# V stationary and two heads on column halves, with the probabilities normalised by GpSimd before they are turned

## The reference

```python
# first block
h = rms_norm(x); qa, ka, va, qb, kb, vb, ga, gb, mg = split(h @ w_in)
ya = banded_attention(qa, ka, va, 128, 1, bias_a, sink) * silu(ga)    # 8 heads, 2 of k and v
yb = sum(alpha[g] * dilated_group(qb[g], kb[g], vb[g]) for g in 3) * silu(gb)   # 8 heads, 3 groups
x = x + (gates[0] * (ya @ w_branch_a) + gates[1] * (yb @ w_branch_b)) @ w_out
# each of two layers
o_nsa  = gs[0] * o_compressed + gs[1] * o_selected + gs[2] * o_window  # 8 heads of 64
o_ret  = silu(g_r) * layernorm(retention(q_r, k_r, v_r)) * gn
o_conv = silu(layernorm(conv31(c_a * sigmoid(c_b))))
x = x + sum(sigmoid(m_g[i]) * (o[i] @ w_branch[i]) for i in 3) @ w_out
x = x + relu(rms_norm(x) @ w_ff1)**2 @ w_ff2
```

## Time and profile before

| | us |
|---|---|
| median of 3 runs (lowest, highest) | 1196.53 (1196.03, 1196.99) |
| the profiled execution | 1196.16 |
| its span, first to last instruction | 1194.4 |
| TensorE busy in it | 1165.7 (98%) |
| VectorE busy | 826.1 (69%) |
| ScalarE busy | 571.1 (48%) |
| GpSimd busy | 46.1 (4%) |

### The profile page before, as it was taken

One profiled execution on the slowest core, in us unless ns is written; L12 is line 12 of the kernel. 1 busy time (PEld: TensorE's weight loads), 2 busy tenths in 40 slices (PEclk: granted clock), 3 DMA queues, 4 the chain that ended last, 5 costly groups with the idle time before them and its releaser, 6 DMA issues.

```text
span 1194.4 us, 17220 instructions
## 1 busy us (share of the span) xinstructions
PE 1165.7 (98%) x6879; PEld 1008.8 (84%) x6879; DVE 826.1 (69%) x1317; ACT 571.1 (48%) x701; POOL 46.1 (4%) x56
## 2 busy tenths in 40 slices
PE   7999999999999999999999999999999999999996
PEld 5888788887898787888999888998778878999885
DVE  4666466557679888787767554699889686777442
ACT  5655565443435666543534433525756534434331
POOL 0232000000000001000000000000000000000000
PEclk9999999999999999999999999999999999999999
DMA  9557555347546666754555565546667654555640
GB/s 310 209 175 247 212 150 177 94 141 264 177 145 211 207 157 191 215 184 161 179 189 178 202 209 178 176 153 214 180 175 214 199 176 147 207 180 188 214 141 36
DMA packets 41344, 219.73 MB, mean 184 GB/s; under 512 B 4311, under 2 KB 14039, under 8 KB 16615
## 3 DMA queue, kind: packets, MB, share of 16 engines
q1 hardware_dynamic: 39104, 204.62, 49.2%
q0 software_dynamic: 1824, 13.78, 6.2%
q10 hardware_dynamic: 336, 0.22, 0.1%
HBM read 217.41 MB, written 1.20 MB: 183 GB/s over the span
## 4 chain that ended last, share of the span: by engine, by line
PE 88%; DVE 4%; ACT 2%; DMA 2%; issue 2%; DVEq 1%; POOLq 0%; POOL 0%; ACTq 0%
PE panel L923 19%; PE panel L925 18%; PE panel L924 18%; PE panel L946 7%; PE panel L945 7%; PE panel L944 7%; PE tile L973 4%; DMA ring_parts<-in_w_layers_dram 2%; DVE ring_parts L613 1%; PE heads_out L1134 1%; ACT ring_parts L571 1%; PE panel L963 1%; PE panel L962 1%; PE panel L961 1%; ACT ring_parts L573 0%
## 5 line engine op out<-in xcount | busy, mean ns | idle before, releaser
L613 DVE TENSOR_TENSOR ring_parts<-ring,ring_parts 128x2048 fp32r<-128x2048 f32 (+1 forms) x173 | 388.1, 2255 | 155.9 <-ACT ring_parts L571 144.6
L571 ACT ACTIVATE ring_parts<-ring 128x2048 fp32r<-128x2048 f32 (+1 forms) x185 | 348.4, 1889 | 260.6 <-PE panel L925 202.3
L923 PE MATMUL panel<-ring_parts,hT_high 128*128 128x512 f32 (+2 forms) x688 | 280.1, 407 | 5.5 <-DMA ring_parts<-in_w_layers_dram 2.4
L925 PE MATMUL panel<-ring_parts,hT_low 128*128 128x512 f32 (+2 forms) x688 | 265.6, 386 | 0.0
L924 PE MATMUL panel<-ring_parts,hT_high 128*128 128x512 f32 (+2 forms) x688 | 264.9, 385 | 0.0
L944 PE MATMUL panel<-hT_high,ring_parts 128*128 128x256 f32 x704 | 199.4, 283 | 0.0
L946 PE MATMUL panel<-hT_high,ring_parts 128*128 128x256 f32 x704 | 199.2, 283 | 0.0
L945 PE MATMUL panel<-hT_low,ring_parts 128*128 128x256 f32 x704 | 199.2, 283 | 0.0
L923 PEld LDWEIGHTS panel<-ring_parts,hT_high 128*128 128x128 f32 x688 | 130.1, 189 | 37.9 <-issue 11.5
L925 PEld LDWEIGHTS panel<-ring_parts,hT_low 128*128 128x128 f32 x688 | 129.9, 189 | 26.9
L923 PE MATMUL panel<-ring_parts,area_parts 128*128 128x512 f32 x384 | 150.6, 392 | 0.0
(11 more groups left out here) (235 smaller groups left out, 1113.9 us busy)
## 6 DMA issues: line engine op xcount, KB each, us to landing
ring<-in_w_layers_dram SPq DMA_DIRECT2D x140, 1024.0 KB, 4.9
ring<-in_w_first_dram SPq DMA_DIRECT2D x40, 1024.0 KB, 5.0
ring_parts<-in_w_layers_dram POOLq DMA_DIRECT2D x12, 1024.0 KB, 8.9
area<-bias_rows SPq DMA_DIRECT2D x16, 160.0 KB, 3.1
ring<-in_w_layers_dram SPq DMA_DIRECT2D x4, 560.0 KB, 3.8
area<-bias_rows SPq DMA_DIRECT2D x16, 96.0 KB, 3.0
area<-bias_rows SPq DMA_DIRECT2D x1, 1536.0 KB, 8.7
area<-in_gains_dram SPq DMA_DIRECT2D x3, 512.0 KB, 5.7
```

Source lines behind the costliest of these rows:

```text
L571: act.activation(ring_lo[:, SLOTS + hi, 0:w], ring[:, slot, 0:w], ACT.Copy).then_inc(high_ready, 1)
L613: g.tensor_tensor(ring_lo[:, slot, 0:w], ring[:, slot, 0:w], ring_lo[:, SLOTS + hi, 0:w], ALU.subtract).then_inc(low_ready, 1)
L923: pe.matmul(ps[:, b, 0:width], high, hi[:, k, :], start=first, stop=False)
L925: mm = pe.matmul(ps[:, b, 0:width], low, hi[:, k, :], start=False, stop=last)
```

## The change

It moves the attention of both kinds to another form, and rewrites both plans.

- *Products.* `outputs_first` and `outputs_layer` do one pair at a time. V is stationary (64 columns), the turned probabilities of up to 256 tokens move, and head i of the pair writes the 64 partitions from 64 i of `heads_out`, now 2 x 256 columns: the output is already turned. `open_group` opens each group with a matmul of zeros over all 512 columns; every product adds to it. A group is 2 pairs in the first block and 4 pairs in a layer, where the selected and window heads of the same four heads and the compressed outputs (`compressed_out(i)`, step O) add to one sum.
- *Normalisation.* GpSimd computes 1/sum by a power, multiplies by the gate (layer) or the row's scale (first block) and scales the probabilities in place, before they are turned. In the first block VectorE scales every second B head (`scale_odd`). TensorE's T waits for `scaled` or `scaled_by_v`. `L` has four slots.
- *Gates and outputs.* In the first block the gates of ga and gb are turned instead of the outputs (step g), kept in x, and multiplied in (`gated_outputs`); x is loaded again later. In a layer step h makes the high and low parts straight from `heads_out`; step y is gone, `sum_out` and `normed_out` too. The compressed probabilities are scaled by VectorE before they are turned (step cmpN).
- *Retention.* Its outputs go to two tiles (Or0, Or1), ScalarE keeps them in SBUF, and VectorE normalises from there. Panels Oc and Or are gone.
- *Order.* In the first block the panel ga moves ahead of vb1, and the wide stage is vb1, vb2, gb, mg0 to mg3: 56 chunks. All chunks of all steps are written out in tables. GpSimd's queue holds scalings and `add_low` in turns (`LOW_ADDED_AT`). The eviction of a wide panel in the first block is done behind chunk 1 of the next.

The diff, cut to its core:

```diff
+FIRST_S = ((0,), (3,), (8,), (12,), (16, 17), (23, 25), (30, 32), (37, 39))
+FIRST_E = (3, 7, 10, 13, 20, 27, 32, 41)
+FIRST_T = ((5, 5), (10, 10), (14, 15), (20, 20), (26, 26), (31, 33), (39, 39), (46, 47))
+FIRST_V = (7, 14, 16, 21, 27, 39, 41, 48)
+FIRST_GATES, FIRST_HIGH = (7, 14, 35, 37), (22, 23, 43, 51)
+LAYER_S = (0, 4, 11, 18, 25, 28, 37, 44)
+LAYER_E = (2, 5, 15, 22, 29, 33, 43, 49)
+LAYER_T = (6, 14, 19, 27, 33, 41, 47, 54)
+LAYER_V = (8, 15, 22, 30, 37, 44, 49, 57)
+LAYER_SUM, LAYER_HIGH = (30, 61), (31, 61)
+LAYER_OTHER = dict(cmpHk=5, cmpFk=8, ro0=10, ro1=7, cmpHv=10, cmpFv=14, rot=17, cmp2=15, cmpS=18, cmpN=19, PcT=22, R0=19, R2=24, Or0=31, Or1=31, oR=51, cv=59, cz=62)
...
+LOW_ADDED_AT = {("vr", 7): "mg0/1", ("mg0", 5): "mg1/1", ("mg1", 7): "mg2/1", ("mg2", 4): "mg3/1", ("mg3", 5): "mg4/1", ("mg4", 4): "mg5/1"}
...
+        def scale_units(g, L, units_of, spans):
+            for u in units_of:
+                for b, at in enumerate(spans):
+                    e = g.tensor_scalar(L[:, u % 4, at], L[:, u % 4, at], coef[:, b, u:u + 1], None, ALU.mult)
+                e.then_inc(scaled, 1)
...
+        def normalise_layer(g, l, p):
...
+            g.wait_ge(probs, l * 16 + (16 + 2 * p + 2))
+            g.tensor_tensor(c, den[:, :, us], minus_one.unsqueeze(2).broadcast_to([P, NB, 2]), ALU.pow)
+            g.drain()
+            g.tensor_tensor(c, c, gt[:, :, :, p // 2, 1 + p % 2], ALU.mult)
+            g.drain()
+            scale_units(g, two("L").rearrange("p (s j) -> p s j", s=4), (2 * p, 2 * p + 1), (slice(0, P), slice(P, 3 * P)))
...
+            def open_group(p, each, base):
+                if p % each:
+                    return
+                if base or p:
+                    pe.wait_ge(group_evicted, base + p // each)
+                pe.matmul(heads_out[:, :, :].rearrange("p c (s t) -> p (c s) t", s=2), zero.broadcast_to([P, P]), ident[:, :].unsqueeze(1).broadcast_to([P, 4, P]),
+                          start=True, stop=False, skip_group_check=True)
...
-                                mm = pe.matmul(heads_out[:, b, hd], PT[:, g, (2 * b + k) * P:(2 * b + k + 1) * P], val,
-                                               start=(g == 0 and k == 0), stop=(g == n - 1 and k == 1))
+                        mm = pe.matmul(heads_out[HD * i:HD * i + HD, p % 2, :], val, PT[:, i, 0, :, k, :], start=False,
+                                       stop=(n == 1 and k == 1), skip_group_check=True)
...
+                            mm = pe.matmul(heads_out[HD * i:HD * i + HD, p % 2, b * P:(b + 1) * P], val, PT[:, i, 1, b, k, :],
+                                           start=False, stop=(k == 1), skip_group_check=True)
...
-                        pe.matmul(heads_out[:, 0, hd], PT[:, 0:P], vsw[:, 0, s:s + HD], start=True, stop=True)
-                        pe.matmul(heads_out[:, 1, hd], PT[:, P:2 * P], vsw[:, 0, s:s + HD], start=True, stop=False)
-                        mm = pe.matmul(heads_out[:, 1, hd], PT[:, 2 * P:3 * P], vsw[:, 1, s:s + HD], start=False, stop=True)
+                                pe.matmul(heads_out[rows, c, :], vsw[:, 0, vals], PT[:, i, 0:TOKENS], start=False, stop=False,
+                                          skip_group_check=True)
...
+                                pe.matmul(heads_out[rows, c, P:TOKENS], vsw[:, 1, vals], PT[:, i, TOKENS:TOKENS + P], start=False,
+                                          stop=False, skip_group_check=True).then_inc(pv_done, 1)
```

More of the change, by code:

```diff
@@ L1678, in _ @@
                             step_layer(*e)
[L1679 removed]
+                        if s == LATE_OUT and waiting:
                             wide_out(waiting)
                             waiting = None
[L1682 to L1685 removed]
+                    if p == "mg5":
                         wide_out(p)
```

665 lines of the change are left out of this document (341 added, 324 removed).

## The result

The changed kernel took 1205.3 us (median of 4 runs, 1204.1 to 1206.6) against 1196.8 us for the kernel before in the same session: ratio 1.0076, 95% interval 1.0064 to 1.0089. It is slower by 8.5 us. The forecast was 1189.4 us with a range of 1182 to 1201: too low by 15.9 us, with the wrong sign, and outside the range. The profiled execution spans 1204.2 us.

A forecast was written before the change was run, and what follows sets the result against it. TensorE's instruction stream, 98% busy, was taken as the bound. 1194.4 - 12.9 + 6.8 - 1.8 - 1.9 - 0.4 + 0.2 + 2.2 + 1.0 = 1187.6 us of span, 1189.4 us forecast, range 1182 to 1201.

The forecast's parts named there:

- What bounds the kernel: Whole kernel: TensorE's instruction stream, busy 98% of the span, sets the time; its three largest waits total 6.0 us.
- the sum: Whole kernel: the span before, 1194.4 us, plus and minus all priced terms, giving 1187.6 us of span.
- br00: End of each layer: br00 may be late behind later convolution transposes and VectorE's low part, +1.0 us in all.
- Products: Attention products on TensorE: two heads run together on column halves, 43.3 us becoming 30.4, a gain of 12.9 us.
- Rival 1: Attention products: column halves don't run together, so -12.9 becomes +7.5 us and the time 1210 us; chance 0.10.
- Zeroing: Opening each group of pairs on TensorE: eight matmuls of zeros at about 0.85 us each, +6.8 us.
- The queue of GpSimd: Additions behind scalings on GpSimd: mg0/1 comes 1.1 us later, +2.2 us for two layers; most others keep their places.
- Small steps and drains: GpSimd's normalisation of a layer pair: 0.5 us for small steps and drains, within 3.1 us of latency.
- GpSimd's scaling: Probabilities scaled on GpSimd: 0.33, 0.46 and 0.74 us for 128, 256 and 512 columns, hidden except at pair 0.
- The wait before R0: TensorE before R0: its 1.9 us wait for VectorE should go, -1.9 us.
- rival 2: Transpositions: GpSimd is late through VectorE's long instructions or half speed; in full +22 us, 1211 us, chance 0.07.
- the mild one: Transpositions: GpSimd late only at the 8 pairs whose exp follows a double rounding, +7, 1197 us; chance 0.13.

The follow-up runs named there:

- experiment 2: The changed kernel without the eight zeroing matmuls, the first product into each region carrying start instead: 1207.0 us.
- experiment 10: The kernel of experiment 8 without the eight zeroing matmuls, the first product into each region carrying start: 1184.1 us.
- experiment 14: The kernel of experiment 12 without zeroing matmuls, only each group's first product carrying start, computation still the reference's: 1179.4 us.
- experiment 7: The changed kernel with GpSimd's drains between normalisation and root steps replaced by semaphores: 1202.0 us.
- experiment 8: The changed kernel with semaphores for GpSimd's drains and three additions per layer earlier in GpSimd's order: 1190.1 us.
- 13: The kernel of experiment 12 with GpSimd's drains put back, all else equal: 1215.0 us.
- experiment 9: The kernel of experiment 8 without GpSimd's scaling of the probabilities: 1181.3 us.
- experiment 12: The kernel of experiment 8 with first-pair transpositions one or two chunks later and the retention's first scores one later: 1183.6 us.
- experiment 3: The changed kernel, drains kept, with three additions per layer moved earlier in GpSimd's order: 1217.6 us.

## Why the prediction was wrong, point by point

- **What bounds the kernel**: right as read, TensorE at 97%. But the step from there to "an edit is worth what it takes out of that stream, plus or minus a few waits" held only as long as the waits stayed few. In the changed kernel they set the pace of the layers (experiment 2). Term by term, its trace gives the 16.6 us by which its span (1204.2) misses the sum (1187.6): waits for additions 3.2 more (7.8 against 2.4 + 2.2), for the scaling 3.5 more (5.0 against 1.3 + 0.2), for ScalarE before R0 3.2, the clock up to 8.5, zeroing 0.8, products -1.1, br00 -1.0, together 17.1. These are the waits as they stand; what their causes are worth is what the runs say, for one wait can stand in for another and can carry a stretch at the lower clock behind it.
- **Products**: right. 29.3 us measured against 30.4, and the matmuls start in twos. Rival 1 is out.
- **Zeroing**: right in size, 6.0 us of 6.8 (experiment 10), 6.7 with what came back (14); by the distance of 0.95 us it is 7.6.
- **The queue of GpSimd: this step failed, and it is the main one.** The forecast put mg0/1 1.1 us later and wrote that "the others keep their places" beside the rounding. Measured in layer 0: mg0/1 was issued 2.5 us later than before (410.86 against 408.34), mg2/1 6.1 us (446.03 against 439.93) and mg3/1 4.1 us (461.53 against 457.38), and against their own negations the three were 9.3, 6.9 and 5.6 us late (7.3 us for the last two in layer 1). For mg0/1 the lateness was more than forecast, but the charge of 2.2 us for it did not come: TensorE waits 1.3 and 0.7 us for it in the two layers, before 1.1 and 1.0. The new waits are for mg2/1, 1.8 and 2.2 us, and for mg3/1, 1.8 us in the second layer. For mg2/1 I named the three chunks and priced them at nothing, and mg3/1, behind the retention's root and pair 5, I didn't look at: its issue in the plan had kept its place, but not what GpSimd does ahead of it. Moving three additions is worth 11.9 us once no drain stands behind them (7 to 8).
- **"Small steps and drains", 0.5 us: failed.** I read a drain as the end of a short operation. It waits for the transfer as well: up to 6.5 us in the changed kernel, worth 3.3 us there (experiment 7) and 31.4 us where additions are early (13). The rows that the forecast chose did not show it, since hardly anything follows an addition there; the trace of before did, in the three rows at the program's start above. Mending the two failed steps together brings 1205.3 - 1190.1 = 15.2 us, against a miss of 15.9; four of the five stretches at the lower clock go with them.
- **GpSimd's scaling: mis-sized, 2 to 3 times.** 0.68, 1.11 and 2.14 us against 0.33, 0.46 and 0.74; the slope was taken from 2 and 16 columns, where the fixed part hides it. The quickest cases are 0.59, 0.91 and 1.56 us. Its price on the time is 8.8 us (experiment 9), against 1.5 in the sum (the old wait of 1.3, and 0.2), and ScalarE's 3.2 us before R0 came on top. What balanced these in experiment 8 are in part charges of the sum that did not come: the 2.2 us for mg0/1, the 2.4 us of old waits for DMA (kept in the sum, gone there), 1.0 for br00, and 1.1 us by which the products were cheaper, 6.7 in all; some 3 to 4 us of the balance I could not place. So the agreement of 1190.1 with 1189.4 is largely luck.
- **The wait before R0**: half right. That for VectorE, 1.9 us, is gone, but 3.2 us for ScalarE took its place, as R0 now shares its chunk with two transpositions, whose copies ScalarE reaches late: in layer 0 it stands 5.3 us just ahead of them, waiting for VectorE, and copies from 416.59; R0 starts at 417.21. One chunk later (12) the wait goes.
- **The clock**: not in the sum at all. Each wait of some length can cost up to 1.7 us more; five such stretches are up to 8.5 us. A forecast of waits must carry this.
- **The rivals**: rival 2, GpSimd late, was the nearest. It named the engine, but placed the damage at the transpositions (5.0 us of waits), not in the transfers (7.8 us) that share the queue. Its full form gave 1211 us at 0.07 and was cut from the range; the mild one gave 1197. Of what it weighed, the slow scaling was true. So was the wait behind VectorE's long instructions, but in few places: in the changed kernel 4 of the 48 scalings of 256 columns take 2.57 to 3.03 us, each with an L638 of VectorE in its time, and one of them is pair 0's, ahead of the 2.8 us for which TensorE waits there. The Trainium skill, GPSIMD Engine Reference, section 4.1, calls one-input work there roughly line-rate: this case's trace does not agree, 2.14 us in the mean for 512 columns on GpSimd, 1.56 at its quickest, against 0.64 us for the same operation on VectorE:

```profile
L1833 DVE TENSOR_SCALAR area<-area,stat 128x512 f32<-128x512 f32 x8 | 4.7, 636 | 3.4 <-POOLq L713 3.4
```

## What to carry to other kernels

When work moves to an idle engine, list what else that engine issues, and for each issue compare its new place with the moment from which it could go, not with its old place; a lightly used queue may carry the transfers on which the busy engine depends. Between dependent steps on a queue that also issues transfers, wait on a semaphore and don't drain. And when a removal from the busiest engine gives nothing, look at which wait grew by the same amount before calling the removed work hidden.

## What the runs showed of the hardware

- A drain on GpSimd behind a transfer that GpSimd issued ends when the transfer has landed: the next operation starts 0.2 us after landing in the three cases shown above (429.2 and 429.40, 453.8 and 454.02, 466.8 and 467.00). In experiment 3 all eight drains of L726 that begin while an addition is under way end 0.07 or 0.08 us after it has landed; in experiment 8 the eight steps in their place start with the transfer still under way. The transfer's own row lasts only 0.9 us. The Trainium skill, Perfetto Trace Analysis, section DMA Instruction — SWDGE (GPSIMD), says that such a row ends when the descriptors are written, not with the data; the trace agrees (0.9 against 7.8 us).
- GpSimd's scaling of a float32 tile in place takes 0.93 us for 256 columns when it is quick, and far longer beside some of VectorE's work. Timeline of GpSimd in experiment 12, twice, then GpSimd and VectorE in the changed kernel:

```profile
149.17 5.73 POOL L706 TENSOR_SCALAR area<-area,stat 128x256 f32<-128x256 f32 x4 [0.21 <-POOL stat L718]
...
160.34 1.86 POOL L706 TENSOR_SCALAR area<-area,stat 128x256 f32<-128x256 f32 x2 [0.21 <-POOL stat L718]
```

```profile
162.50 5.74 POOL L698 TENSOR_SCALAR area<-area,stat 128x256 f32<-128x256 f32 x4 [0.21 <-issue]
```

```profile
164.32 2.31 DVE L638 TENSOR_TENSOR ring_parts<-ring,ring_parts 128x2048 fp32r<-128x2048 f32 x1
```

  Two take 1.86 us; four take 5.7 and not 3.7 when one of VectorE's instructions with two operands from SBUF lies in their time. By single instructions of the second case, three take 0.92 or 0.94 us and one, which starts with L638, takes 3.03; the 40 of 48 that meet no L638 in the changed kernel take 0.91 to 1.21. That this instruction holds GpSimd is argued from the rows; no run took it away.
- Matmuls on column halves with float32 run side by side as those on row halves do, at nearly the same price: 1.22 us for eight of 256 columns, against 1.27.
- After a wait of TensorE, the granted clock can be 0.5 for 3.4 us (6.8 in experiment 10) although TensorE is busy again. It need not be: no such stretch stands at the 2.1 us wait of experiment 12, and one stands behind the 2.9 us wait at the same place in experiment 14.
